# One weight chunk of projections moved between the heads of a sparse attention, linear attention moved one chunk earlier

## The chip, the cores and the metric

The kernel runs on one core of one Trainium2 chip. The core has five engines that run side by side and meet only at semaphores: TensorE (PE, with its weight loads listed as PEld), VectorE (DVE), ScalarE (ACT), GpSimd (POOL) and SyncE (SP), which issues most of the DMAs. The metric is the device time of one launch in microseconds (us); of several launches the median counts. Lower is better.

## The reference, cut to what matters

256 tokens of width 1024 pass through two blocks. Each block is a token mixer with a residual, and a mixture of 32 experts with a residual. Only the mixer of the first block is touched here:

```
hn = rms_norm(x, g_mix)
proj = hn @ w_in            # qa ka va ra alr | qb kb vb | qi ki wi | gate_a gate_b (1024 columns each)
ya = gla_mixer(qa, ka, va, ra, alr, ...) @ w_br_gla      # linear attention, 4 heads, 4 chunks of 64 tokens
yb = dsa_mixer(norm(qb), norm(kb), vb, qi, ki, wi, rel_bias) @ w_br_att   # sparse attention, 8 heads
mixed = sigmoid(gate_a) * ya + sigmoid(gate_b) * yb
x = x + mixed @ w_out
x = x + hier_moe(rms_norm(x, g_ffn), ...)
```

The linear attention has a state per chunk of tokens: the keys are decayed, k_dec^T v is formed for each chunk (the updates), the states are a running sum of the updates with a decay, and the outputs are q times the states, normed per head and multiplied by silu(ra). The sparse attention adds a bias by relative position and a mask of the 64 best keys to the scores, and takes a softmax over them.

## The kernel before, in words

Everything is float32. Each engine has its own program, written out by hand, and waits for named semaphores; there is no scheduler. Weights stream through a ring of six slots of 2 MB (`ring`), loaded by SP in one fixed order (`load`, issued at line 399); a load waits until the slot's last reader has passed (`s_used`). PE releases a slot with the first matmul that follows the last reader (`read[0]` in `mm`), so a slot comes free only when that next matmul has run. Three later loads go into the arena instead of the ring, and stand in the same SP order: w_gate of the second group of four experts waits for `s_gtp`, w_up of it for `s_on`, w_down of it for `s_mix`.

The projections of the first block come in chunks of 512 columns (numbers CH_QB to CH_GATE + 3). A gate chunk (`gate_chunk`) is 32 matmuls of 128x128 weights by 256 tokens; the profile lists each float32 matmul as two records, so 64. Its result fills two banks of PSUM (0 and 1, or 2 and 3), and ACT writes the sigmoid of it to `gate_a` or `gate_b` (line 851). The order on PE (lines 1882 to 1948) is:

- the chunk RA, gate chunk 0 (CH_GATE), the updates of the linear attention (waits for `s_kdec`), gate chunk 1, the outputs of the linear attention (waits for `s_st`, the states), gate chunk 2, the transposes of the normed outputs (waits for `s_gn`), gate chunk 3, the head transposes of the sparse attention's q and k, a wait for their copies (`s_hT_a`, `s_hT_d`) and for the last sigmoid, and the sparse attention.

The sparse attention is a loop over 16 (tile, head) pairs on PE, DVE and ACT. In step i PE makes the scores of pair i, transposes the probabilities of pair i - 2, runs what `beside_sparse(i)` puts there, and multiplies the probabilities of pair i - 3 by v. The piece beside is the product of the linear attention with w_br_gla (`gla_branch`): 24 of its 32 matmuls lie in the 16 steps, so one and two in turn, and 8 behind the loop. They write banks 6 and 7 or 3 and 4 by `beside_buf`; DVE multiplies each pair of results by `gate_a` (`mix_gla`, line 1309), two of the four inside the loop (behind its steps 7 and 12).

ACT's order is written out as well. After the silu of RA (line 841) ACT waits for `s_rel_dram`, which comes when a DMA that ACT issued at line 834 has landed: it writes a row of bias values, held in 8 partitions of SBUF, 128 times over to a scratch tensor in DRAM (2 MB). ACT then issues the two DMAs that read the bias back in its skewed form (line 846, `s_bias`), and takes the square root for the head norm (`root(ROOTS["dsa"])`, line 662). Only then come the sigmoids of the gate chunks.

DVE's order around this: the selection of the keys (`select(1)`), the decayed keys (line 1280, `s_kdec`), the norm of q and k of the sparse attention (`group_norm("dsa")`, lines 989, 990, 939, then 942 to 945 and 993 behind ACT's root), the states of the linear attention (lines 1289 and 1292, `s_st`), the norm of the linear attention's outputs (`group_norm("gla")`, the same lines, then 1302, `s_gn`), the copy of kT (line 1305), the loop of the sparse attention. POOL adds the masks to the bias when both bias DMAs have landed (line 609).

Behind the first mixer stand the out-product, router and experts of block one (lines 1175, 1181, 784 belong to them), then block two. Its experts have 6 MB of weights each.

Of the kernel before, what the change touches and what calls it, by code (L numbers as in the profile page):

```python
# [27 lines left out]
ACT = mybir.ActivationFunctionType  # L28
AX = mybir.AxisListType

P = 128
T, D = 256, 1024
TT = T // P
KD = D // P
# [81 lines left out]
def program(nc, a, out):  # L116

    with ExitStack() as ctx:
# [3 lines left out]
        def sem(name):  # L122
            return ctx.enter_context(nc.semaphore(name))
# [92 lines left out]
        def bank(b, n=512, o=0):  # L216
            return ps[:, b * 512 + o:b * 512 + o + n]
# [74 lines left out]
        s_otp = sem("out_transposed")  # L292
        s_oT = sem("out_T")
        s_br = sem("branch_product")
        s_mix = sem("branch_mixed")
# [61 lines left out]
        def slot3(s, k, n):  # L357
            return place(s)[:, 0:k * n].rearrange("p (k n) -> p k n", k=k)
# [158 lines left out]
        def tiles4(b0, n=4):  # L517

            return ps[:, b0 * 512:b0 * 512 + n * T].rearrange("p (m t) -> p m t", t=T)
# [9 lines left out]
        def beside_buf(i):  # L529

            return (6, 3)[i % 2]

# [124 lines left out]
        def _(act):  # L657
# [189 lines left out]
            root(ROOTS["dsa"])  # L847
            for n in range(4):
                gate = (gate_a, gate_b)[n // 2][:, 4 * (n % 2):4 * (n % 2) + 4, :]
                act.wait_ge(s_proj, CH_GATE + n + 1)  # L850
                act.activation(gate, tiles4(2 * ((CH_GATE + n) % 2)), ACT.Sigmoid).then_inc(s_pev_a, 1)
                if n == 1:
                    act.wait_ge(s_go, 1)
                    for i in range(2):
                        act.activation(og.rearrange("p t (n i e) -> p t n i e", n=2, i=2)[:, :, :, i],
                                       bank(6 + i).rearrange("p (t n e) -> p t n e", t=TT, n=2),
                                       ACT.Copy).then_inc(s_gog, 1)
                    root(ROOTS["gla"])
                if n == 2:
                    act.wait_ge(s_gtp, 1)  # L860
                    act.activation(gla_T, tiles4(4), ACT.Copy, scale=gcol[:, R_GLA:R_GLA + 1]).then_inc(s_gT, 1)
# [4 lines left out]
            act.wait_ge(s_otp, 1)  # L866
            act.activation(att_T, tiles4(4), ACT.Copy).then_inc(s_oT, 1)  # L867
            norm(1, R_FFN)
            act.wait_ge(s_rexp_in, 1)
# [52 lines left out]
        def _(dve):  # L922
            done = [0]

            def step(ins):

                done[0] += 1
                ins.then_inc(s_dve, 1)
                dve.wait_ge(s_dve, done[0])
# [377 lines left out]
            def mix_gla(n):  # L1307
                dve.wait_ge(s_br, n + 1)
                dve.tensor_tensor(mixT[:, 2 * n:2 * n + 2, :], tiles4(beside_buf(n), 2),
                                  gate_a[:, 2 * n:2 * n + 2, :], ALU.mult).then_inc(s_mix, 1)  # L1310

            def beside_sparse(i):
                if i in (7, 12):
                    mix_gla((7, 12).index(i))

# [3 lines left out]
            for n in range(4):  # L1319
                dve.wait_ge(s_br, 4 + n + 1)  # L1320
                gb = gate_b[:, 2 * n:2 * n + 2, :]
                step(dve.tensor_tensor(gb, tiles4(n, 2), gb, ALU.mult))
                dve.wait_ge(s_mix, n + 1)
                dve.tensor_tensor(mixT[:, 2 * n:2 * n + 2, :], mixT[:, 2 * n:2 * n + 2, :], gb,
                                  ALU.add).then_inc(s_mix, 1)
# [91 lines left out]
        def _(pe):  # L1417
# [477 lines left out]

            gate_chunk(CH_GATE)

            pe.wait_ge(s_kdec, 1)
# [9 lines left out]
            ins.then_inc(s_u, 1)  # L1908
            gate_chunk(CH_GATE + 1)
            pe.wait_ge(s_st, 1)  # L1910
# [6 lines left out]
            ins.then_inc(s_go, 1)  # L1917
            gate_chunk(CH_GATE + 2)
            pe.wait_ge(s_gn, 1)
            transposes(4, lambda m, tt: og[:, tt, m * P:(m + 1) * P], 4, s_gtp, 4)  # L1920
            gate_chunk(CH_GATE + 3)
            pe.wait_ge(s_hn, 1)
            pe.wait_ge(s_gT, 1)
            pe.wait_ge(s_gog, 2)
            head_transposes(q_tm, k_tm)
            pe.wait_ge(s_hT_a, 1)
            pe.wait_ge(s_hT_d, 1)
            pe.wait_ge(s_pev_a, CH_GATE + 4)
            w_bg = slot3(CH_BG, 4, D)

            def gla_branch(m, k):

                n = m // 2
                if m % 2 == 0 and k == 0 and n >= 2:
                    pe.wait_ge(s_mix, n - 1)
                ins = mm(bank(beside_buf(n), T, (m % 2) * T), w_bg[:, k, m * P:(m + 1) * P], gla_T[:, k, :], k == 0,
                         k == 3)
                if m % 2 == 1 and k == 3:
                    ins.then_inc(s_br, 1)

            def beside_sparse(i):

                if i < 16:
                    for t in range(i * 24 // 16, (i + 1) * 24 // 16):
                        gla_branch(t // 4, t % 4)

            arrived(CH_BG, 0)
            sparse_attention(beside_sparse)
            for m in (6, 7):
                for k in range(4):  # L1950
                    gla_branch(m, k)
            read[0] += 1
            pe.wait_ge(s_on, 2)
# [111 lines left out]
```

## Time and profile before

| | us |
|---|---|
| median of 3 runs | 1020.8 |
| lowest and highest run | 1019.43, 1023.84 |
| the profiled execution, its own time | 1014.91 |
| its span, first to last instruction | 1013.1 |
| PE busy in the span | 831.0 (82%) |
| DVE, ACT, POOL busy | 208.4, 172.4, 56.7 |
| mean granted clock of TensorE | 0.935 |

Times in the views are counted from the start of the span. "Busy" is time in instructions. A row of a timeline is a run of like instructions of one engine: start, length, engine, line, operation, written tile <- read tiles, shapes, count, and in brackets how long the engine sat idle before it and what ended that. A row of the stretches (A:B) gives for each engine its busy time and count, then the clock granted to TensorE as a share of full speed, the share of the DMA engines that was busy, and GB/s. SPq and ACTq are the issuing of DMAs on these engines' queues.

### The profile page before, as it was taken

What the parts mean: (1) busy time and instruction counts of PE and PEld (TensorE: products, weight loads), DVE (VectorE), ACT (ScalarE), POOL (GpSimd) and SP (SyncE); (2) the same over time, 40 slices, a digit from 0 to 9 for tenths busy, and PEclk for the clock granted to TensorE, in tenths of its full rate; (3) what the DMA queues carried; (4) which work ended last, traced back from release to release, by engine and by line L of the source; (5) the groups of instructions that cost most, each with busy time, mean ns of one, the idle gap of its engine ahead of it and who ended that gap; (6) DMA issues with size and microseconds to landing.
All of it is one profiled execution on the core that took longest, in us unless ns stands there. A gap on an engine that the chain in (4) does not pass through costs nothing.

```text
span 1013.1 us, 18784 instructions
## 1 busy us (share of the span) xinstructions
PE 831.0 (82%) x8295; PEld 536.5 (53%) x8295; DVE 208.4 (21%) x545; ACT 172.4 (17%) x386; POOL 56.7 (6%) x60
## 2 busy tenths in 40 slices
PE   5999999999989998999999896856657565675755
PEld 4546488776576665444665754452525334253541
DVE  2023515122332222044444210100001010010100
ACT  2012112330411114011653110001001000000100
POOL 8000003000002000043000000000000000000000
PEclk9999999999999999999999899888978798897978
DMA  9944675526276999444264899999999999999995
GB/s 268 368 167 150 109 234 184 217 91 241 89 289 262 407 408 388 175 167 166 83 234 161 320 426 413 426 423 421 428 411 429 418 427 421 419 427 412 433 415 205
DMA packets 67184, 307.30 MB, mean 303 GB/s; under 512 B 4528, under 2 KB 7688, under 8 KB 58952
## 3 DMA queue, kind: packets, MB, share of 16 engines
q1 hardware_dynamic: 62544, 301.85, 75.2%
q10 hardware_dynamic: 3256, 3.67, 2.2%
q0 software_dynamic: 1344, 1.20, 0.5%
q8 instruction: 30, 0.49, 0.2%
q14 instruction: 10, 0.08, 0.0%
HBM read 303.56 MB, written 3.15 MB: 303 GB/s over the span
## 4 chain that ended last, share of the span: by engine, by line
PE 59%; DMA 32%; SPq 3%; DVE 2%; ACT 2%; issue 1%; DVEq 0%; ACTq 0%
PE ps L1422 56%; DMA ring<-in_w_down 14%; DMA ring<-in_w_up 10%; DMA ring<-in_w_gate 7%; SPq L399 3%; PE ps L1448 1%; DMA xx<-in_x 1%; PE ps L1582 0%; PE ps L1545 0%; PE ps L1470 0%; DVE arena L1181 0%; ACT arena L784 0%; DVE xx L1209 0%; DVE xs L950 0%; ACT arena L720 0%
## 5 line engine op out<-in xcount | busy, mean ns | idle before, releaser
L1422 PE MATMUL ps<-ring,arena 128*32 128x128 f32 (+2 forms) x5520 | 290.5, 353 | 145.7 <-DMA ring<-in_w_down 61.4
L1422 PEld LDWEIGHTS ps<-ring,arena 128*32 128x32 f32 (+1 forms) x5520 | 179.7, 123 | 249.0 <-issue 91.2
L1422 PE MATMUL ps<-ring,xx 128*128 128x512 f32 (+2 forms) x416 | 167.0, 560 | 0.0
L1422 PE MATMUL ps<-arena 128*32 128x128 f32 (+10 forms) x752 | 117.2, 358 | 5.4 <-ACT arena L791 1.7
L1422 PEld LDWEIGHTS ps<-ring,xx 128*128 128x128 f32 x416 | 77.0, 193 | 84.3 <-issue 83.3
L1422 PEld LDWEIGHTS ps<-arena 128*128 128x128 f32 (+4 forms) x752 | 64.7, 154 | 39.1 <-issue 32.5
L1422 PE MATMUL ps<-xx,ring 128*128 128x256 f32 (+2 forms) x400 | 78.2, 382 | 0.0
L1422 PEld LDWEIGHTS ps<-xx,ring 128*128 128x128 f32 (+2 forms) x400 | 64.7, 175 | 12.9 <-issue 1.6
L1175 DVE TENSOR_TENSOR arena<-arena,ps 128x128 f32<-128x128 f32 x40 | 11.5, 288 | 282.5 <-ACT arena L771 282.5
L1422 PE MATMUL ps<-arena,xs 128*128 128x128 f32 x512 | 64.7, 287 | 1.9 <-DVE arena L1081 1.9
L1422 PEld LDWEIGHTS ps<-arena,xs 128*128 128x128 f32 x512 | 61.6, 201 | 6.7 <-issue 4.2
L771 ACT ACTIVATE arena<-ps 128x128 f32<-128x128 f32 x40 | 11.1, 278 | 306.8 <-PE ps L1422 306.8
L1193 DVE COPY arena<-ps 128x512 f32<-128x512 f32 x16 | 11.1, 692 | 171.8 <-PE ps L1422 171.8
L791 ACT ACTIVATE arena<-ps 128x512 f32<-128x512 f32 x16 | 9.6, 597 | 159.2 <-PE ps L1422 159.2
L1422 PE MATMUL ps<-arena,ring 128*128 128x256 f32 x128 | 30.9, 382 | 1.2 <-ACT arena L867 1.2
L1181 DVE TENSOR_TENSOR arena<-ps,gcol 128x512 f32<-128x512 f32 x32 | 22.1, 692 | 37.6 <-PE ps L1422 37.6
L1422 PE MATMUL ps<-ring,xs 128*128 128x512 f32 x64 | 27.8, 592 | 0.0
L1422 PEld LDWEIGHTS ps<-arena,ring 128*128 128x128 f32 x128 | 23.3, 194 | 4.0 <-issue 1.4
L1422 PEld LDWEIGHTS ps<-ring,xs 128*128 128x128 f32 x64 | 12.1, 190 | 14.4 <-issue 14.3
L1702 PE MATMUL ps<-const,arena 128*128 128x128 f32 x40 | 13.7, 343 | 4.4 <-DVE arena L1175 4.0
L1448 PE MATMUL ps<-const,xs 128*128 128x128 f32 x32 | 5.6, 346 | 12.4 <-DVE xs L950 12.4
L609 POOL TENSOR_TENSOR arena<-arena 128x1024 f32<-128x1024 f32 (+1 forms) x2 | 7.8, 3918 | 136.2 <-DMA arena<-bias_scratch 136.2
(246 smaller groups left out, 514.8 us busy)
## 6 DMA issues: line engine op xcount, KB each, us to landing
ring<-in_w_gate SPq DMA_DIRECT2D x38, 2048.0 KB, 22.8
ring<-in_w_up SPq DMA_DIRECT2D x38, 2048.0 KB, 23.1
ring<-in_w_down SPq DMA_DIRECT2D x37, 2048.0 KB, 24.2
ring<-in_w_in SPq DMA_DIRECT2D x16, 2048.0 KB, 18.5
ring<-in_w_out SPq DMA_DIRECT2D x4, 2048.0 KB, 7.9
arena<-in_w_gate SPq DMA_DIRECT2D x2, 2048.0 KB, 10.3
arena<-in_w_up SPq DMA_DIRECT2D x2, 2048.0 KB, 9.1
arena<-in_w_down SPq DMA_DIRECT2D x2, 2048.0 KB, 7.8
```

The lines of the kernel that those rows point to most:

```text
L399: sp.dma_start(dst, src).then_inc(s_extra[s] if s < 0 else s_slot[s % RING], 16)
L609: pool.tensor_tensor(bm[tt], bm[tt], pick_mask[:, tt:tt + 1, 0:nk].broadcast_to([P, AH, nk]), ALU.add).then_inc(s_bm, 1)
L771: act.activation(silu_g[:, j % 2], bank(6, P), ACT.Silu).then_inc(s_silu[b], 1)
L791: act.activation(y_sb[:, 0:512], bank(4), ACT.Copy).then_inc(s_ysb_a[b], 1)
L1175: dve.tensor_tensor(hid_tm[:, j % 2], silu_g[:, j % 2], bank(7, P), ALU.mult).then_inc(s_h[b], 1)
L1181: dve.tensor_tensor(xg[:, 4 * half:4 * half + 4, :], bank(6 + half).rearrange("p (k s) -> p k s", k=4), gains, ALU.mult).then_inc(s_xg[b], 1)
L1193: dve.tensor_copy(y_sb[:, 512:1024], bank(5)).then_inc(s_ysb_d[b], 1)
L1422: ins = pe.matmul(dst, w, x, start=start, stop=stop, skip_group_check=True)
L1448: ins = pe.transpose(bank(b0 + m // 2, P, (m % 2) * T + tt * P), src(m, tt), ident)
L1702: pe.transpose(bank(4, P, j * P), hid_tm[:, j % 2], ident).then_inc(s_ht[b], 1)
```

## The change

The last gate chunk (gate chunk 3) leaves its place ahead of the head transposes. 8 of its 32 matmuls run behind the head transposes, ahead of the wait for the copies of q and k; the other 24 run in steps 0 to 7 of the sparse attention, three in each. The 24 matmuls of the linear attention's product that were spread over the 16 steps are now in steps 8 to 15, three in each. The gate's results are written to bank 3 and bank 6, copied raw to `gate_b` by DVE behind its steps 4 and 9, and turned into a sigmoid by ACT in place, after the transposed attention output. The two multiplications by gate_a in the loop move to DVE's steps 12 and 15. The updates of the linear attention run ahead of gate chunk 0 instead of behind it, its outputs ahead of gate chunk 1, its transposes ahead of gate chunk 2. On ACT the copies of the linear attention's outputs stand behind the sigmoid of gate chunk 0, and that of the transposed ones behind gate chunk 1. SP's program is not touched.

```diff
@@ buffers of the pieces beside the heads
-            return (6, 3)[i % 2]
+            return (3, 6)[i % 2]
@@ ACT
-            for n in range(4):
+            for n in range(3):
                 gate = (gate_a, gate_b)[n // 2][:, 4 * (n % 2):4 * (n % 2) + 4, :]
                 act.wait_ge(s_proj, CH_GATE + n + 1)
                 act.activation(gate, tiles4(2 * ((CH_GATE + n) % 2)), ACT.Sigmoid).then_inc(s_pev_a, 1)
-                if n == 1:
+                if n == 0:
                     act.wait_ge(s_go, 1)
...
                     root(ROOTS["gla"])
-                if n == 2:
+                if n == 1:
                     act.wait_ge(s_gtp, 1)
                     act.activation(gla_T, tiles4(4), ACT.Copy, scale=gcol[:, R_GLA:R_GLA + 1]).then_inc(s_gT, 1)
...
             act.activation(att_T, tiles4(4), ACT.Copy).then_inc(s_oT, 1)
+            act.wait_ge(s_gcp, 2)
+            act.activation(gate_b[:, 4:8, :], gate_b[:, 4:8, :], ACT.Sigmoid).then_inc(s_pev_a, 1)
@@ DVE
+            def copy_gate(half):
+                if half == 0:
+                    dve.wait_ge(s_gate, 1)
+                else:
+                    dve.wait_ge(s_proj, CH_GATE + 4)
+                dve.tensor_copy(gate_b[:, 4 + 2 * half:6 + 2 * half, :],
+                                tiles4(beside_buf(half), 2)).then_inc(s_gcp, 1)
+
             def beside_sparse(i):
-                if i in (7, 12):
-                    mix_gla((7, 12).index(i))
+                if i in (4, 9):
+                    copy_gate((4, 9).index(i))
+                if i in (12, 15):
+                    mix_gla((12, 15).index(i))
...
                 dve.wait_ge(s_br, 4 + n + 1)
                 gb = gate_b[:, 2 * n:2 * n + 2, :]
+                if n == 2:
+                    dve.wait_ge(s_pev_a, CH_GATE + 4)
@@ PE
-            gate_chunk(CH_GATE)
-
             pe.wait_ge(s_kdec, 1)
...
             ins.then_inc(s_u, 1)
-            gate_chunk(CH_GATE + 1)
+            gate_chunk(CH_GATE)
             pe.wait_ge(s_st, 1)
...
             ins.then_inc(s_go, 1)
-            gate_chunk(CH_GATE + 2)
+            gate_chunk(CH_GATE + 1)
             pe.wait_ge(s_gn, 1)
             transposes(4, lambda m, tt: og[:, tt, m * P:(m + 1) * P], 4, s_gtp, 4)
-            gate_chunk(CH_GATE + 3)
+            gate_chunk(CH_GATE + 2)
...
             head_transposes(q_tm, k_tm)
-            pe.wait_ge(s_hT_a, 1)
-            pe.wait_ge(s_hT_d, 1)
-            pe.wait_ge(s_pev_a, CH_GATE + 4)
+            arrived(CH_GATE + 3, 0)
+            w_gate3 = slot3(CH_GATE + 3, KD, 512)
             w_bg = slot3(CH_BG, 4, D)
 
+            def last_gate(t):
+
+                m, k = t // KD, t % KD
+                ins = mm(bank(beside_buf(m // 2), T, (m % 2) * T), w_gate3[:, k, m * P:(m + 1) * P], xnT[:, k, :], k == 0,
+                         k == KD - 1)
+                if (m, k) == (1, KD - 1):
+                    ins.then_inc(s_gate, 1)
+                if (m, k) == (3, KD - 1):
+                    ins.then_inc(s_proj, 1)
+
             def gla_branch(m, k):
 
                 n = m // 2
-                if m % 2 == 0 and k == 0 and n >= 2:
-                    pe.wait_ge(s_mix, n - 1)
+                if m % 2 == 0 and k == 0:
+                    if n < 2:
+                        pe.wait_ge(s_gcp, n + 1)
+                    else:
+                        pe.wait_ge(s_mix, n - 1)
...
             def beside_sparse(i):
 
                 if i < 16:
-                    for t in range(i * 24 // 16, (i + 1) * 24 // 16):
-                        gla_branch(t // 4, t % 4)
-
+                    for t in range(3 * i, 3 * i + 3):
+                        if t < 24:
+                            last_gate(8 + t)
+                        else:
+                            gla_branch((t - 24) // 4, (t - 24) % 4)
+
+            pe.wait_ge(s_pev_a, CH_GATE + 3)
+            for t in range(8):
+                last_gate(t)
+            pe.wait_ge(s_hT_a, 1)
+            pe.wait_ge(s_hT_d, 1)
             arrived(CH_BG, 0)
             sparse_attention(beside_sparse)
...
-            read[0] += 1
+            read[0] += 2
```

## Rows read from the trace of the kernel before

**Rows 1.** Page: the chain that ended last, by engine; then a piece of it.

```profile
PE 59%; DMA 32%; SPq 3%; DVE 2%; ACT 2%; issue 1%; DVEq 0%; ACTq 0%
...
189.97 1.15 issue
```

**Rows 2.** Timeline of PE from RA's end to the first head.

```profile
129.02 13.98 PE L1422 MATMUL ps<-xx,ring 128*128 128x256 f32 x64
142.93 1.15 PE L1422 MATMUL ps<-arena 64*64 64x128 f32 x32
...
158.02 1.16 PE L1422 MATMUL ps<-arena 64*64 64x128 f32 x32
...
187.71 1.91 PE L1448 MATMUL ps<-const,arena 128*128 128x128 f32 x16
191.12 0.46 PE L1422 MATMUL ps<-arena 64*128 64x128 f32 x2 [1.50 <-issue]
```

**Rows 3.** Timeline of DVE: head norm behind the root, states, norm of the linear outputs.

```profile
148.76 0.35 DVE L942 RECIPROCAL stat<-stat 128x32 f32<-128x32 f32 x1 [21.98 <-ACT stat L662]
...
152.49 2.26 DVE L1292 SCALAR_TENSOR_TENSOR arena<-arena,stat,ps 128x128 f32<-128x128 f32 x6
160.34 2.53 DVE L989 TENSOR_TENSOR xs<-arena 128x1024 f32<-128x1024 f32 x1 [5.59 <-ACT arena L855]
...
164.17 3.13 DVE L939 TENSOR_SCALAR stat<-stat 128x32 f32<-128x32 f32 x1
167.59 0.35 DVE L942 RECIPROCAL stat<-stat 128x32 f32<-128x32 f32 x1 [0.30 <-ACT stat L662]
...
169.91 1.23 DVE L1302 TENSOR_TENSOR arena<-arena 128x1024 f32<-128x1024 f32 x1
```

**Rows 4.** Timeline of ACT and its queue: the bias DMAs, the load ahead of the root.

```profile
146.17 1.01 ACTq L846 DMA_DIRECT2D arena<-bias_scratch  x2
147.21 1.28 ACT L662 ACT_TABLE_LOAD   x1 [16.96 <-issue]
```

**Rows 5.** Stretch with the bias write alone in flight; columns as in rows 7.

```profile
104.00:108.00 4.00, 4.00 (x10) 1.71 (x9) 0.00 (x0) 0.00 (x0) 0.00 (x0) 1.00 0.46 49
```

**Rows 6.** Timeline of PE in the loop: the transposes that begin steps 10, 11, 12.

```profile
210.27 0.44 PE L1545 MATMUL ps<-const,arena 128*128 128x128 f32 x2
...
212.09 0.44 PE L1545 MATMUL ps<-const,arena 128*128 128x128 f32 x2
...
214.34 0.44 PE L1545 MATMUL ps<-const,arena 128*128 128x128 f32 x2
```

**Rows 7.** The loop: us, then PE, PEld, DVE, ACT, POOL busy, clock, DMA share, GB/s.

```profile
191.10:219.70 28.60, 28.58 (x153) 21.91 (x153) 8.01 (x36) 12.60 (x49) 0.00 (x0) 1.00 0.32 131
```

**Rows 8.** Timeline of PE: the same work after a pause, and without one.

```profile
12.40 3.65 PE L1448 MATMUL ps<-const,xs 128*128 128x128 f32 x16 [12.40 <-DVE xs L950]
...
16.70 1.27 PE L1422 MATMUL ps<-xx,ring 128*128 128x256 f32 x3
...
279.67 5.47 PE L1422 MATMUL ps<-arena,xs 128*128 128x128 f32 x32 [0.96 <-DVE arena L1081]
...
293.25 3.84 PE L1422 MATMUL ps<-arena,xs 128*128 128x128 f32 x32
```

**Rows 9.** A stretch behind that pause; columns as in rows 7.

```profile
282.00:283.00 1.00, 1.00 (x7) 1.00 (x7) 0.38 (x3) 0.00 (x0) 0.00 (x0) 0.50 1.01 406
```

**Rows 10.** Timeline of POOL: the masks added to the bias.

```profile
159.45 7.81 POOL L609 TENSOR_TENSOR arena<-arena 128x1024 f32<-128x1024 f32 x2 [136.22 <-DMA arena<-bias_scratch]
```

**Rows 11.** Timeline of SP's queue, and PE's first use of expert weights.

```profile
188.02 0.37 SPq L399 DMA_DIRECT2D ring<-in_w_up  x1
...
285.91 3.70 PE L1422 MATMUL ps<-ring,arena 128*32 128x128 f32 x128 [0.56 <-DVE arena L1181]
```

**Rows 12.** Waits: engine, line, what it waited for, us in total, times, longest.

```profile
ACT arena L735 <- DVE xx L1331: 27.2, 1, 27.2
```

**Rows 13.** The chain in order of time, late in the run: start, us, what.

```profile
628.69 24.09 DMA ring<-in_w_up
```

More of the change, by code:

```diff
@@ L293, in program @@
         s_oT = sem("out_T")
+        s_gate = sem("first_half_of_last_gate")
+        s_gcp = sem("last_gate_copied")
         s_br = sem("branch_product")
```

## The prediction

> **What bounds the kernel now.** I read the chain that ended last first. PE holds 59% of it and DMA 32%, all others little [rows 1]. The DMA part lies in the second block's experts, where pieces like one of 24.09 us stand in the chain [rows 13]; ahead of them PE's own work is the chain. Those late loads start when PE frees their slots, so a time that PE loses or wins in the first mixer, at 129 to 230 us, should reach the end whole. Next I read PE's timeline of the part that is reordered. From 129.02 PE runs without a gap through the gate chunks and the two small products of the linear attention at 142.93 and 158.02; the one idle time is 1.50 us ahead of the first head at 191.12 [rows 2]. It is a piece of the chain: 1.15 us of it has no work behind it at all [rows 1]. Then the loop: 28.58 of 28.60 us of PE busy [rows 7]. So there is nearly nothing to fill on PE, and the question is what the new order makes PE wait for. That needs the timelines of DVE and ACT. DVE sits idle for 21.98 us, up to 148.76, waiting for ACT's square root, and makes the states of the linear attention only behind that, up to 152.49 + 2.26 = 154.75 [rows 3]. ACT in turn is idle for 16.96 us ahead of the load for that root, and leaves when it can issue the bias reads at 146.17 [rows 4], which is when the bias write has landed. Before, PE asks for the states at 158.02, 3.2 us after they are there: the late root costs nothing.
>
> **The updates, ahead of gate chunk 0.** They need the decayed keys; DVE had been idle since 126.8 when the root came [rows 3], so these were done before RA ended at 129.02. The updates keep their 1.15 us and do not wait. Nothing won, nothing lost.
>
> **The outputs, one chunk sooner.** PE will be ready for them at 129.02 + 1.15 + 13.91 (gate chunk 0, from 129.02 to 142.93 in rows 2) = 144.1. The states come at 154.75, plus 0.1 for the semaphore. Nothing in the change moves the write of the bias, ACT's order ahead of the root, or DVE's order. PE stands still for **10.8 us**. Queued behind this wait is everything: gate chunk 1 and 2, the transposes, the heads. DVE and ACT have nothing to do either in that time that they had not before. The write runs at 49 GB/s with 0.46 of the engines even when it is alone [rows 5], so it does not profit from an emptier queue; the one load that is now later, the first of w_out (its slot is freed by the first output matmul), overlapped it for the last 3 us only. I bound that gain by 0.4 us and take none.
>
> **The clock.** The pause is longer than any that I find inside this mixer. What pauses do: behind an idle time of 0.96 us ahead of 279.67 [rows 8], and others just before it, the granted clock was 0.50, the 1.2 GHz level [rows 9], and 32 records took 5.47 us against 3.84 for the same work later [rows 8], so 1.63 us were lost. After 12.40 us of idle at the start, 16 transposes took 3.65 us [rows 8] against 1.91 [rows 2], and matmuls still took 1.27 us for 3 at 16.70 where 64 take 13.98; full speed came at about 17.1. That is 1.74 for the transposes and some 0.65 for three matmuls: 2.4. The new pause is nearest to this one, so I take **2.4 us**, with 1.6 as the lower bound and twice 2.4 as the upper. The Trainium skill, in TensorE: Matmul & The Clock Gate, section Part 1: The HAM clock gate, has the half clock as the default state that activity lifts, which speaks against any change that makes a pause; the trace agrees, and the page's way of costing it, half of the slow time, gives the same order.
>
> **The norm of the linear outputs.** PE finishes gate chunk 1 at 154.85 + 1.16 + 13.98 + 2.4 = 172.4 and then waits for it. ACT copies the outputs from about 156.1 on (158.4 with the slow clock), and DVE starts at about 158.5 instead of 160.34. From DVE's start to its end it took 10.8 us [rows 3]; two pieces of it, 2.53 us for the multiplication and 3.13 us for an operation on 32 values, were long because POOL was adding the masks just then, from 159.45 for 7.81 us [rows 10]. With one load less ahead of them the bias reads land earlier, between 155 and 159.5. If POOL starts just ahead of DVE the whole 7.81 us fall on it: 158.3 + 7.8 + 1.2 + 1.2 + 0.5 + 3.55 (from the reciprocal at 167.59 to the end at 171.14) = 172.6. So this wait is 0 to 0.2 us, **0** in the sum; if the clock did not fall it would be up to 2.6 instead of the 2.4 of the clock, not on top of it. The Trainium skill, in SBUF — State Buffer, section SBUF: two separate sides, says that DVE and POOL take their shared port as a lock for a whole instruction; the two long DVE pieces agree, each ending as a POOL addition ends. By that rule the bound just given is the worst, and the sum stays as it is.
>
> **The last gate chunk.** PE does the same 32 matmuls elsewhere. Removed from its place: 13.8 us. 8 of them behind the head transposes cost 8 x 0.437 = 3.5 us (13.98 for 64 records, 32 matmuls, [rows 2]) and cover the 1.50 us idle time: kT's copy, which PE waited for, is then done. Gain **1.5 us**. The other 24 in the loop: a step with one matmul beside takes 212.09 - 210.27 = 1.82 us, one with two 214.34 - 212.09 = 2.25 [rows 6], so one more costs 0.43, its full price; nothing in a step hides it. 24 x 0.43 = 10.3, and 3.5 + 10.3 = 13.8: a move at no gain. The lower bound of what the loop hides is 0.02 us [rows 7].
>
> **What goes with it.** DVE gets two copies of some 0.7 us in the loop and is busy for 8.01 of 28.60 us there [rows 7]; PE waits for the first from step 8 on, DVE makes it in step 4; the second is made in step 9 for step 10 or 11. Behind each copy on DVE stand the next logits, due two steps later. Cost 0; without this cover, 1.4. ACT's one sigmoid and its table load, some 2.3 us (1.28 for a load in rows 4), lie ahead of ACT's next norm, for which it waited 27.2 us [rows 12], and DVE needs the result only for its third product, behind half of the attention's branch. Cost 0. SP: the slot of the last gate chunk comes free only behind the loop, so the load of w_up that went out at 188.02, and behind it in SP's order the second w_gate, go out at about 234. The experts use them from 285.91 on [rows 11], then 12 us later; 8 MB are queued there, some 20 us at the 406 GB/s of rows 9. Cost 0; 40 us of cover.
>
> **Sum.** + 10.8 + 2.4 - 1.5 = **+11.7 us**. The profiled execution, 1014.9, would become 1026.6. It lies 5.9 us below the median of the runs, 1020.8, with the same program; I add the difference to the median: **1032.5 us**, 1.1% slower.
>
> **Rivals.**
> 1. The clock stays low for longer, since the output products are small: twice the price, +14.1, 1034.9. For it: no row shows a restart on small products. Against it: each slow stretch that I read ended by itself under 5 us of work.
> 2. The loop hides the 24 matmuls (waits between engines take in the time): + 11.7 - 10.3 = +1.4, 1022.2, no change. It decides if a step with three matmuls beside takes less than 2.25 + 0.43. Against it: rows 6 and 7.
> 3. The other side: the states are there in time. If the bias write landed 10.8 us sooner than here, near 135, PE would never wait; left is the gain at the heads, -1.5, 1019.3, not slower. It is a single place, ACT's wait at line 842; each us by which the write is early takes one from the pause. For it: one execution is a thin base. Against it: the rate of 49 GB/s looks fixed, and it began before anything that the change touches.
> 4. Both, 2 and 3: -11.8, 1009.0, faster.
> 5. The change doesn't do what it says: the chunk's matmuls would have to stand elsewhere on PE, which its program excludes; no chance of its own.
>
> **How the numbers follow.** Forecast 0.78, rival 1 0.09, rival 2 0.06, rival 3 0.05, rival 4 0.02. A measurement of this kernel can tell about 0.5%, 5.1 us, from no change. Slower by more: forecast and rival 1, 0.87. Within it: rivals 2 and 3, 0.11. Faster by more: 0.02. The range has to hold 8 in 10: the forecast with its bounds (stall 10.4 to 10.8, clock 1.6 to 2.4) is +10.5 to +11.9, rival 1 reaches +14.1, and the medians of runs that spread over 4.4 us add about 3 on each side. 1027 to 1038.
>
> **What would show it.** Right: PE idle for 10 to 11 us ahead of the output products, ended by DVE's line of the states; the clock at 0.50 behind it; no idle time ahead of the first head; the loop at 28.6 + 10.3 = 38.9 us; DVE still idle for 22 us up to about 148.8. Wrong: PE's outputs starting before 150, or a loop of under 36 us, or the part from RA's end to the loop's end less than 9 us longer than its 90.6 us. If that part is 11 us longer but the end is not, the step that failed is that PE's delay reaches the end whole.

## The result and the profile after

| | before | after |
|---|---|---|
| median of 16 runs each, us | 1020.33 (1014.85 to 1023.84) | 1027.32 (1025.11 to 1029.73) |
| ratio, 95% interval | | 1.0076 [1.0059, 1.0092] |
| profiled execution, us | 1014.9 | 1029.73 |
| its span, us, and mean granted clock | 1013.1 | 1027.9, 0.928 |
| RA's end to the start of the attention's branch, us | 96.2 | 109.4 |

The kernel is slower, by 7.0 us at the median (the interval is 6.0 to 9.4 us) where 11.7 were forecast; the time lies 0.3 us above the low end of the range. Lines of the new kernel are numbered higher: the matmul helper is L1438 (L1422), the states L1296 (L1292), the root L664 (L662). In the kernels of the experiments they stand some 4 to 8 lines further down: the matmul helper is L1446 in the variants of the changed kernel and L1430 in those of the kernel before, the states are L1304 and L1300.

The page of the changed kernel, its span and its chain by engine:

```profile
span 1027.9 us, 18788 instructions
...
PE 53%; DMA 38%; DVE 2%; SPq 2%; ACT 2%; issue 1%; ACTq 0%; DVEq 0%
```

PE held 59% of the chain before and DMA 32% [rows 1]. The bias write has entered the chain, and PE follows behind it. The chain of the changed kernel in order of time, two of its links:

```profile
99.92 48.51 DMA bias_scratch<-arena
...
157.10 17.84 PE ps L1438 x96
```

The timeline of PE in the changed kernel, RA's end to the first steps behind the heads (start, us, instructions, idle time before and what ended it):

```profile
130.00 1.15 PE L1438 MATMUL ps<-arena 64*64 64x128 f32 x32
131.09 14.08 PE L1438 MATMUL ps<-xx,ring 128*128 128x256 f32 x64
157.10 2.04 PE L1438 MATMUL ps<-arena 64*64 64x128 f32 x32 [11.93 <-DVE arena L1296]
159.07 15.88 PE L1438 MATMUL ps<-xx,ring 128*128 128x256 f32 x64
174.78 1.04 PE L1464 MATMUL ps<-const,arena 128*128 128x128 f32 x8
...
191.22 3.62 PE L1438 MATMUL ps<-xx,ring 128*128 128x256 f32 x16
194.76 0.49 PE L1438 MATMUL ps<-arena 64*128 64x128 f32 x2
```

Read it against rows 2. The updates stand right behind RA, as forecast, and do not wait; behind gate chunk 0 PE is idle for 11.93 us, ended by DVE's line of the states. The output products take 2.04 us instead of 1.16, the next chunk 15.88 instead of 13.98. The transposes of the linear outputs at 174.78 don't wait. The eight matmuls of the last chunk stand at 191.22 and the first head follows with no idle time. The clock and the traffic behind the pause, then the loop, as rows 7 give them (us; PE, PEld, DVE, ACT, POOL; clock; DMA share; GB/s):

```profile
160.00:161.00 1.00, 1.00 (x4) 0.74 (x3) 0.70 (x1) 0.98 (x2) 1.00 (x1) 0.50 0.97 358
161.00:163.00 2.00, 2.00 (x7) 1.61 (x6) 2.00 (x1) 0.57 (x1) 2.00 (x1) 0.56 1.05 410
163.00:170.00 7.00, 7.00 (x34) 6.17 (x33) 6.00 (x9) 1.51 (x2) 0.14 (x1) 1.00 0.30 110
194.80:233.70 38.90, 38.90 (x201) 30.96 (x201) 9.21 (x38) 12.43 (x48) 0.00 (x0) 1.00 0.06 22
```

The granted clock is at 0.50, the 1.2 GHz level, until about 162.8 (worked out from the 0.56 of 161 to 163), and full from then on. The loop holds 38.90 us of PE without a gap.

What DVE and ACT did meanwhile (timelines of the changed kernel):

```profile
151.05 0.35 DVE L946 RECIPROCAL stat<-stat 128x32 f32<-128x32 f32 x1 [23.38 <-ACT stat L664]
...
154.78 2.27 DVE L1296 SCALAR_TENSOR_TENSOR arena<-arena,stat,ps 128x128 f32<-128x128 f32 x6
160.30 3.92 DVE L993 TENSOR_TENSOR xs<-arena 128x1024 f32<-128x1024 f32 x1 [3.26 <-ACT arena L857]
...
168.31 1.23 DVE L1306 TENSOR_TENSOR arena<-arena 128x1024 f32<-128x1024 f32 x1
```

```profile
148.45 1.02 ACTq L848 DMA_DIRECT2D arena<-bias_scratch  x2
149.50 1.28 ACT L664 ACT_TABLE_LOAD   x1 [18.36 <-issue]
```

This is rows 3 and 4 again. The states end at 157.05, 2.3 us later than before, because the write landed 2.3 us later: it was issued 0.6 us later and took 48.51 us, against 46.9 (99.28 to 146.17) before. All of the 13.2 us that the part from RA's end to the branch is longer is now named: 11.93 of pause, 0.88 + 1.80 of low clock (against 1.16 and the 14.08 that the chunk ahead of the pause took), less 1.5 at the heads, is 13.1. The delay reaches the end: the span is 14.8 us longer.

### The profile page after: what moved, and what is told of

It is laid out like the page before. It is cut to its first block, busy times and chain, and to the rows that moved or that the text cites. A ratio compares the mean times of both kernels' runs of the same rounds, so it can differ in the third digit from the quotient of the medians.

```text
span 1027.9 us, 18788 instructions
## 1 busy us (share of the span) xinstructions
PE 836.2 (81%) x8295; PEld 541.2 (53%) x8295; DVE 208.0 (20%) x547; ACT 173.6 (17%) x387; POOL 55.7 (5%) x60
## 4 chain that ended last, share of the span: by engine, by line
PE 53%; DMA 38%; DVE 2%; SPq 2%; ACT 2%; issue 1%; ACTq 0%; DVEq 0%
PE ps L1438 50%; DMA ring<-in_w_up 14%; DMA ring<-in_w_down 14%; DMA bias_scratch<-arena 5%; DMA ring<-in_w_gate 5%; SPq L401 2%; PE ps L1464 1%; DMA xx<-in_x 1%; PE ps L1598 0%; PE ps L1561 0%; PE ps L1486 0%; ACT arena L786 0%; DVE xx L1213 0%; DVE xs L954 0%; ACT arena L722 0%
## 5 line engine op out<-in xcount | busy, mean ns | idle before, releaser
L1438 PE MATMUL ps<-ring,arena 128*32 128x128 f32 (+2 forms) x5520 | 288.1, 351 | 143.1 <-DMA ring<-in_w_down 60.2
L1438 PEld LDWEIGHTS ps<-ring,arena 128*32 128x32 f32 (+1 forms) x5520 | 178.9, 122 | 244.8 <-issue 92.3
L1438 PE MATMUL ps<-ring,xx 128*128 128x512 f32 (+2 forms) x416 | 170.9, 570 | 0.0
L1438 PE MATMUL ps<-arena 128*32 128x128 f32 (+10 forms) x752 | 118.5, 374 | 17.9 <-DVE arena L1296 11.9
L1438 PEld LDWEIGHTS ps<-ring,xx 128*128 128x128 f32 x416 | 78.8, 198 | 86.2 <-issue 85.3
L1438 PEld LDWEIGHTS ps<-arena 128*128 128x128 f32 (+4 forms) x752 | 66.4, 162 | 51.5 <-issue 32.7
L1438 PE MATMUL ps<-xx,ring 128*128 128x256 f32 (+2 forms) x400 | 80.7, 386 | 0.0
L1438 PEld LDWEIGHTS ps<-xx,ring 128*128 128x128 f32 (+2 forms) x400 | 65.1, 178 | 12.7 <-issue 1.3
L1438 PE MATMUL ps<-arena,xs 128*128 128x128 f32 x512 | 64.4, 286 | 1.8 <-DVE arena L1085 1.8
L1438 PEld LDWEIGHTS ps<-arena,xs 128*128 128x128 f32 x512 | 61.3, 200 | 5.8 <-issue 3.4
L1438 PE MATMUL ps<-arena,ring 128*128 128x256 f32 x128 | 29.4, 380 | 1.2 <-ACT arena L869 1.2
L1438 PE MATMUL ps<-ring,xs 128*128 128x512 f32 x64 | 27.8, 592 | 0.0
L1438 PEld LDWEIGHTS ps<-arena,ring 128*128 128x128 f32 x128 | 23.7, 191 | 4.2 <-issue 1.4
L1438 PEld LDWEIGHTS ps<-ring,xs 128*128 128x128 f32 x64 | 12.1, 190 | 14.4 <-issue 14.3
```

Source lines behind the costliest of these rows:

```text
L1438: ins = pe.matmul(dst, w, x, start=start, stop=stop, skip_group_check=True)
```

## The experiments

Two theories stood against each other. **R** (late root): ACT waits for the bias write ahead of a square root that has nothing to do with it, so the states come at a fixed time, and PE, now earlier, waits. Its rival puts the loss in the placement: outputs between the chunks, the slow clock itself, or the loop. A second pair was about size: **C**, that the kernel before pays for its 1.50 us pause ahead of the heads [rows 2] with more than its length, in granted clock, against the plain sum. All experiments hold each engine's count of expert rounds, which is read from memory, at 1 or more, by one register operation per engine. The kernel before and the changed one with that alone show what it costs. The cuts of the edits below leave it out; they are against the changed kernel, or against the kernel before where the heading names it.

**The kernel before, again.** Expected:

> The kernel before, with one register operation per engine more: the count of rounds that is read from memory is held at 1 or above (all kernels of these experiments have it). Expected by every theory: ratio 1.000 within 0.3%, PE idle 1.5 us ahead of the first head and 0 ahead of the output products. It is also a second look at the kernel before: its profiled execution was at 1015 while its median is at 1020. If the bias write lands later in the slower executions (theory L), the states come up to 3 us later there with no pause on PE; if it is the late weight stream that varies (theory W), everything up to the end of the sparse loop agrees with the first profile within 1 us and the difference lies behind 600 us.

Measured: 1020.17 us (1014.63 to 1023.67), ratio 1.0001 [0.9976, 1.0026]. The register operation costs nothing that shows. The profiled execution took 1023.57 us with a span of 1021.7, 8.6 us above that of the other. The difference is mostly clock. Nearly the same work of the second block, in both (a stretch of the kernel before, then of the kernel before again):

```profile
496.10:506.10 10.00, 10.00 (x73) 7.62 (x71) 5.39 (x30) 7.85 (x32) 0.00 (x0) 1.00 0.02 5
```

```profile
498.50:508.50 10.00, 10.00 (x47) 8.26 (x46) 3.11 (x21) 4.77 (x23) 0.00 (x0) 0.55 0.19 79
```

PE is busy in all of both, but does 47 instructions in place of 73. By the timelines of PE the same instructions stand 0.8 us later in the second execution at RA's end, 2.4 us behind the first block's attention, 4.1 near 480, 8.7 at 509, and the spans differ by 8.6. The steps lie where the clock is at 0.50 in the second execution alone: 3.4 us behind 193, 3.4 us near 406, and some 10 us from 497 to 507, which cost 1.6, 1.7 and 4.6 us. So such a stretch costs about half its length. The first of them lies just behind the short pause (timeline of PE, then a stretch, kernel before again):

```profile
191.89 0.46 PE L1430 MATMUL ps<-arena 64*128 64x128 f32 x2 [1.50 <-issue]
```

```profile
194.00:195.00 1.00, 1.00 (x4) 0.53 (x2) 0.00 (x0) 0.25 (x2) 0.00 (x0) 0.50 1.00 406
```

So the kernel before is a mixture: of 96 executions of it, 35 lie under 1017 us and 58 at 1019 or above. The profiled execution that the prediction was made against belongs to the first group, the median to the second. Neither theory of the expectation explains it: the bias reads went out 1.25 us later (147.42 against 146.17), with no pause ahead of the output products, and the difference lies ahead of 600 us.

**The changed kernel, again** (one execution). Expected:

> The changed kernel, a second profile. Theory R (the late root on ScalarE, behind the bias write, makes the states late): a pause of 10.5 to 12.5 us ahead of the output products, the clock at 0.50 behind it, the part from RA's end to the loop's end 102 to 104 us. The rival (the pause of the first profile was a chance of one execution): a pause under 8 us.

Measured: 1024.98 us, span 1023.2. In the timeline of PE the pause is 10.35 us, just under the 10.5 expected at least, and the slow clock behind it costs 1.4 us:

```profile
154.70 2.04 PE L1446 MATMUL ps<-arena 64*64 64x128 f32 x32 [10.35 <-DVE arena L1304]
156.67 14.63 PE L1446 MATMUL ps<-xx,ring 128*128 128x256 f32 x64
```

The bias reads went out at 146.06 here, and the outputs start 8.64 us behind that; in the first execution it was 148.45 and 8.65. So the pause ends with the landing of the write, some 8.65 us behind it.

**Root first.** The direct test of R: the same work, the root ahead of the wait for the write.

```diff
             act.activation(ra, ..., ACT.Silu).then_inc(s_pev_a, 1)
+            root(ROOTS["dsa"])
             act.wait_ge(s_rel_dram, 16)
...
-            root(ROOTS["dsa"])
             for n in range(3):
```

> The changed kernel with ScalarE's square root for the head norm put ahead of its wait for the bias write instead of behind it. Theory R: the states are ready near 139, no pause ahead of the output products, the clock stays at 1.00, so 10.8 to 11.9 us of pause and 2.4 to 2.7 us of slow clock go; a new wait for the norm of the linear outputs of 0 to 5 us can take their place, because VectorE's norm then meets GpSimd's masks. From RA's end to the loop's end 89 to 94 us; 9 to 14 us faster than the changed kernel, ratio to before 0.998 to 1.003. The rival (VectorE's own work or the updates make the states late, not the root): the pause keeps 8 us or more and the ratio stays at 1.0076.

Measured: **1013.65 us** (1009.39 to 1021.09), ratio to before 0.9943 [0.9917, 0.9970]; 13.7 us below the changed kernel, and faster than both kernels. The gain on the changed kernel is as expected; the ratio lies below the 0.998 to 1.003 that was. The timelines of PE and of DVE:

```profile
130.19 14.08 PE L1446 MATMUL ps<-xx,ring 128*128 128x256 f32 x64
144.20 1.15 PE L1446 MATMUL ps<-arena 64*64 64x128 f32 x32
145.28 14.08 PE L1446 MATMUL ps<-xx,ring 128*128 128x256 f32 x64
```

```profile
131.81 0.35 DVE L952 RECIPROCAL stat<-stat 128x32 f32<-128x32 f32 x1 [5.04 <-ACT stat L668]
...
135.53 2.27 DVE L1304 SCALAR_TENSOR_TENSOR arena<-arena,stat,ps 128x128 f32<-128x128 f32 x6
```

The states end at 137.8, PE asks at 144.2, the pause is gone, and with it the slow products. RA's end to the branch is 94.7 us: 96.2 less the 1.5 of the heads. By that plain sum the median would be 1.5 us under the kernel before; it is 6.6 under it.

**The early root in the kernel before.** If the root were worth something by itself, it would show here.

```diff
+            root(ROOTS["dsa"])
             act.wait_ge(s_rel_dram, 16)
...
-            root(ROOTS["dsa"])
             for n in range(4):
```

> The kernel before with ScalarE's root ahead of its wait for the bias write, the fourth corner of the square of both orders on both engines. Theory R: the states are ready 12 to 14 us earlier, near 146 behind the updates of 143, but PE asks for them at 158 as before, so nothing moves on PE: from RA's end to the attention's branch 96.2 to 98 us, ratio 0.998 to 1.002. The rival (the early root by itself is what made the mended kernel faster than before): ratio 0.996 or less.

Measured: 1020.52 us (1014.68 to 1031.03), ratio 1.0000 [0.9973, 1.0027]. Timelines of DVE and of PE:

```profile
145.22 2.26 DVE L1300 SCALAR_TENSOR_TENSOR arena<-arena,stat,ps 128x128 f32<-128x128 f32 x6
```

```profile
158.65 1.15 PE L1430 MATMUL ps<-arena 64*64 64x128 f32 x32
...
191.75 0.46 PE L1430 MATMUL ps<-arena 64*128 64x128 f32 x2 [1.50 <-issue]
```

The states end at 147.5, some 7 us sooner than in rows 3 (they now wait for the updates), but PE asks at 158.65 as before; the 1.50 us pause stayed. RA's end to the branch took 99.4 us, 3.1 more than in rows 2, because the clock is at 0.50 from about 193 to 199, behind that pause. With the three kernels above this closes a square: the early root is worth 0 within 2.8 us in the old order and 13.7 us in the new one. R is shown.

**The gate chunk moved, the linear attention where it was.** The half of the change that fills the pause at the heads, without the half that makes the new one.

```diff
-                if n == 0:
+                if n == 1:
                     act.wait_ge(s_go, 1)
...
-                if n == 1:
+                if n == 2:
                     act.wait_ge(s_gtp, 1)
...
+            gate_chunk(CH_GATE)
             pe.wait_ge(s_kdec, 1)
...
-            gate_chunk(CH_GATE)
+            gate_chunk(CH_GATE + 1)
             pe.wait_ge(s_st, 1)
...
-            gate_chunk(CH_GATE + 1)
+            gate_chunk(CH_GATE + 2)
             pe.wait_ge(s_gn, 1)
             transposes(...)
-            gate_chunk(CH_GATE + 2)
             pe.wait_ge(s_hn, 1)
```

> One part of the change alone: the last gate chunk between the heads, its sigmoid behind them, but the updates, outputs and transposes of the linear attention behind gate chunks 0, 1 and 2 as before. Theory R: PE asks for the states at 158 as before, no pause there, no slow clock; 1.5 us won ahead of the first head, 1 to 1.5 us lost where the head transposes now follow directly on the linear attention's and wait for their copy. Ratio 0.998 to 1.002, loop 38.9 us, RA's end to the loop's end 89.5 to 91 us. The rival (three matmuls beside each head are what costs): this kernel is as slow as the changed one, 1.006 or more.

Measured: 1015.14 us (1011.96 to 1016.71), ratio 0.9952 [0.9928, 0.9976], below the 0.998 to 1.002 expected. The rival fell: the three matmuls beside each head fill the loop as in the changed kernel, and the kernel is not slow. RA's end to the branch took 96.2 us, no less than before: it wins the 1.50 us at the heads and pays for a new short wait a little earlier, behind the transposes of the linear outputs (timeline of PE):

```profile
159.01 1.15 PE L1446 MATMUL ps<-arena 64*64 64x128 f32 x32
...
174.01 1.04 PE L1472 MATMUL ps<-const,arena 128*128 128x128 f32 x8
...
176.34 1.94 PE L1472 MATMUL ps<-const,arena 128*128 128x128 f32 x16 [1.29 <-issue]
```

Yet the median fell by 5.1 us, and none of 11 executions reached 1019. In this kernel a pause of nearly the same length, followed by other work, does not bring the upper group. The plain sum has no room for that.

**The pause filled with spare work.** This parts the pause from its clock. PE gets 24 matmuls whose result nobody reads.

```diff
             gate_chunk(CH_GATE)
+            for k in range(24):
+                mm(bank(6, T), xnT[:, k % KD, 0:P], xnT[:, k % KD, :], True, True)
             pe.wait_ge(s_st, 1)
```

> The changed kernel with 24 spare matmuls of 128x128 by 256 (10.5 us, results unused) between gate chunk 0 and the wait for the states. The pause is full of work now, but the states come no earlier. Theory K (of the changed kernel's loss, 1.4 to 2.7 us are the half clock behind the pause): the outputs take 1.16 us instead of 2.04, gate chunk 1 takes 14.0 instead of 14.6 to 15.9, from RA's end to the attention's branch 104.5 to 106 us instead of 106.5 and 109.4, ratio to before 1.004 to 1.006. The rival (the slow stretch comes from something other than the pause): both stay as slow as in the changed kernel, and the ratio stays at 1.0076 or above.

Measured: 1024.48 us (1021.35 to 1028.98), ratio 1.0061 [1.0036, 1.0085], 2.8 us below the changed kernel (1.8 if each is taken against the kernel before as measured beside it, 1019.28 and 1020.33). Timeline of PE:

```profile
145.79 10.52 PE L1446 MATMUL ps<-xx 128*128 128x256 f32 x48
156.24 1.15 PE L1446 MATMUL ps<-arena 64*64 64x128 f32 x32
157.32 14.08 PE L1446 MATMUL ps<-xx,ring 128*128 128x256 f32 x64
```

The spare work stands in place of the idle time, so all that can be saved is the clock: the outputs take 1.15 us in place of 2.04, the chunk 14.08 in place of 15.88 or 14.63. RA's end to the branch is 105.1 us, and 96.2 + 10.5 - 1.5 is 105.2. In this execution the states were ready at 154.6, some 1.6 us before the spare work ended, so the pause would have been 8.8 us and the filling gave part of the clock's gain away.

This trace holds something else that bears on C. Near 510 the clock is at 0.50 for about 10 us, at the same work as in the kernel before again, though PE has no idle time ahead of the outputs or of the heads here (a stretch of it):

```profile
510.00:511.00 1.00, 1.00 (x6) 0.97 (x5) 0.00 (x0) 0.42 (x3) 0.00 (x0) 0.50 0.00 0
```

It is the longest execution of this kernel, 4.5 us above its median. The long stretch near 500 does not need idle time of PE ahead of the heads.

**The short pause of the kernel before, filled**, measured twice. The test of C:

```diff
             head_transposes(q_tm, k_tm)
+            for k in range(4):
+                mm(bank(2, T), xnT[:, k, 0:P], xnT[:, k, :], True, True)
             pe.wait_ge(s_hT_a, 1)
```

> The kernel before with 4 spare matmuls (1.75 us, results unused) in its one pause, the 1.50 us ahead of the first head. In the second profile of the kernel before the clock fell to 0.50 at 193.7 just behind this pause and the loop took 1.6 us more; in the first it did not. Theory C (the median of before holds such a slow stretch, and the two kernels that lose the pause win it back on top of their 1.5 us): the loop never slows, ratio 0.997 to 0.999. The rival (the pause is harmless and the wins of 5 us have their source behind the mixer): ratio 1.000 to 1.001.

> The kernel before with its short pause filled, measured once more since its interval reached 1.0001. Theory C: ratio 0.996 to 0.999, no or nearly no executions above 1019 where about two in three of the kernel before are. The rival: ratio 0.999 to 1.001 with the same share of slow executions as before.

Measured: 1015.54 us, ratio 0.9977 [0.9952, 1.0001], and 1015.87 us, ratio 0.9975 [0.9952, 0.9999]. The timeline of PE and the stretch behind it, in the first of them:

```profile
190.09 1.89 PE L1430 MATMUL ps<-xx 128*128 128x256 f32 x8
191.91 0.48 PE L1430 MATMUL ps<-arena 64*128 64x128 f32 x2
```

```profile
194.00:195.00 1.00, 1.00 (x6) 0.55 (x5) 0.05 (x1) 0.31 (x2) 0.00 (x0) 1.00 1.01 410
```

The spare work takes 1.89 us where the idle time took 1.50, so by the plain sum this kernel is 0.4 us slower. It is 3.6 to 3.7 us faster at the median and 2.3 to 2.4 at the mean, and of its 24 executions none reached 1019, where 58 of 96 of the kernel before did. The intervals end at 1.0001 and 0.9999; the missing upper group is the stronger evidence. But the filled kernel is not the lower group alone: 6 of its 24 executions lie at 1017.5 to 1018.3, where the kernel before has 1 of 96. In the two executions that were profiled the clock is full where it was 0.50 above, in the attention and around 500 us. They are two of the 24, and the mean granted clock of all 24 is 0.930, while in the 80 executions of the kernel before whose clock is on record it is 0.934 under 1017 us and 0.927 at 1019 or above. That the filling takes time off is shown; that it does so through the stretches near 500 is not.

**The short pause put back**, in the changed kernel and in the one with the root first: the two waits of the first head stand again ahead of the eight matmuls.

```diff
-            for t in range(8):
-                last_gate(t)
             pe.wait_ge(s_hT_a, 1)
             pe.wait_ge(s_hT_d, 1)
+            for t in range(8):
+                last_gate(t)
```

> The changed kernel with the wait for the copies of q and k back ahead of the 8 matmuls of the last gate chunk, so that the pause of 1.5 us ahead of the heads is there again; the long pause ahead of the outputs stays. Theory C (that short pause costs more than its length in most executions, through the clock here and later in the run; this is why the changed kernel lost 7 us and not the 11.7 of the forecast): median 3 to 5 us above the changed kernel's 1027.3, ratio 1.010 to 1.013. The rival (the short pause costs its 1.5 us, and the difference to the forecast lies elsewhere): 1028 to 1029, ratio 1.009.

> The same for the changed kernel with the early root, which has no pause in the mixer at all (median 1013.7, ratio 0.9943). Theory C: the short pause takes back most of its 5.8 us, median 1017 to 1020, ratio 0.998 to 1.001, with executions above 1019. The rival: 1.5 us more, median 1015, ratio 0.996.

Measured: 1029.6 us (1028.44 to 1037.15) in six runs, ratio 1.0136 [1.0088, 1.0184]; and 1014.54 us (1012.77 to 1017.57), ratio 0.9965 [0.9940, 0.9989]. Timeline of PE, root first with the pause:

```profile
175.10 3.69 PE L1446 MATMUL ps<-xx,ring 128*128 128x256 f32 x16 [1.54 <-DVE arena L1317]
```

The pause is back at 1.54 us, and with the root first it costs 0.9 us, or 1.6 with each taken against the kernel before as measured beside it; C had it bring several. C as it was stated, that any such pause ahead of the heads brings the upper group, fell. In both kernels the eight matmuls, products of 256 columns, follow the pause; in the kernel before it is the first head's small products (64 rows, 128 columns). The changed kernel with the pause is slower by 2.3 us (3.1 in the same way), but on six runs, two of which lie at 1036 and above; its interval holds both what C and what the rival expected, and I read nothing from its size. The kernel that would tell, the pause directly ahead of the first head in the new order, was not tried.

## Why the prediction was right in sign and too high in size

- **The late root decides: right.** It named DVE's states behind ACT's root behind the bias write, and a pause of 10.8 us. Three executions show 11.93, 10.35 and, with the short pause put back, 8.84 us (timeline below). The chunk between took 14.08 us and the outputs began 8.65 us behind the bias reads in all three; what moves is the landing of the write, 146.06 or 148.45, and RA's end, 129.3 to 130.8. So the stated bounds, 10.4 to 10.8, held in none of the three.

```profile
154.71 2.04 PE L1446 MATMUL ps<-arena 64*64 64x128 f32 x32 [8.84 <-DVE arena L1304]
156.68 16.10 PE L1446 MATMUL ps<-xx,ring 128*128 128x256 f32 x64
```

- **Clock behind the pause, 2.4 us: right in kind and size, not in its bounds.** 2.7 and 1.4 in the two executions of the changed kernel, 2.9 behind the 8.84 us above, where 1.6 to 2.4 were the bounds; between the medians 1.8 to 2.8 when the pause was filled. The price does not go with the length of the pause. Rival 1, 4.8, did not occur. One of the rows that it was priced from, the start of the kernel [rows 8], has long durations only: the stretches of that time list the clock at 1.00. The Trainium skill, in TensorE: Matmul & The Clock Gate, section Part 1: The HAM clock gate, has activity lift the half clock; the spare matmuls, whose results nobody reads, agree: 1.15 us for the outputs behind them, 2.04 behind idle time.
- **Norm of the linear outputs, 0: right.** It ended at 169.5, PE asked at 174.8. The collision with POOL stayed inside its bound. Timeline of POOL in the changed kernel:

```profile
156.34 6.80 POOL L611 TENSOR_TENSOR arena<-arena 128x1024 f32<-128x1024 f32 x2 [133.13 <-DMA arena<-bias_scratch]
```

  DVE's multiplication began inside it, at 160.30, and ended at 164.22, 1.08 us behind it, 3.92 us long; with the root first, where DVE was done before POOL began, the same one took 1.23. The prediction has both long DVE pieces of the kernel before end as an addition ends. Only the second did; the multiplication ended at 162.87, 1.07 us behind the end of the first addition (159.45, 2.35 us long), so it seems to have begun to run there. The Trainium skill, in SBUF — State Buffer, section SBUF: two separate sides, has the port as a lock for a whole instruction, and this agrees.
- **The loop hides nothing: right.** Three matmuls beside a step give steps of 2.69 us where the forecast was 2.25 + 0.43, and 38.90 us where 38.9 were forecast. Rivals 2 and 4 fell with this. Timeline of PE, the transposes of three steps, to be held against rows 6:

```profile
224.40 0.44 PE L1561 MATMUL ps<-const,arena 128*128 128x128 f32 x2
...
227.09 0.44 PE L1561 MATMUL ps<-const,arena 128*128 128x128 f32 x2
...
229.77 0.44 PE L1561 MATMUL ps<-const,arena 128*128 128x128 f32 x2
```

- **Late weights, the copies, the sigmoid, 0: right.** Timeline of SP's queue and of PE at the first expert:

```profile
237.52 0.37 SPq L401 DMA_DIRECT2D ring<-in_w_up  x1
```

```profile
300.96 3.70 PE L1438 MATMUL ps<-ring,arena 128*32 128x128 f32 x128 [0.56 <-DVE arena L1185]
```

  The load went out 49.5 us later than in rows 11 and PE came there 15.05 us later, and its wait is the same 0.56 us.
- **The delay reaches the end: right** in the pair of profiled executions, with 13.2 us at the branch, 15.05 at the first expert and 14.8 in the span.
- **The states in time (rival 3): did not occur by itself,** and root first is that case made on purpose. It was priced at -1.5 and gave -6.6 at the median.
- **The step that was off: "I add the difference to the median".** The sum was made against one execution of 1014.9 us and laid onto a median of 1020.8 as if both stood for the same program at the same clock. The sentence in the prediction even gives the 5.9 us between them, and asks nothing of it. Against the group of executions to which the profiled one belongs, near 1015, the changed kernel costs 12.3 us, and 11.7 were forecast; but that group is picked after the result, and set against all executions of the changed kernel. Against the median it costs 7.0. The mis-sized term is **"Gain 1.5 us"** at the heads: it is 1.5 by the timeline (94.7 against 96.2), and filling the same pause in the kernel before took off 3.7 us more with spare work that is 0.4 us longer than the idle time, so 4.1 beyond the plain sum. +10.8 + 2.4 - 1.5 - 4.1 is +7.6, with 7.0 measured. The 4.1 is carried over from another kernel: in the new order, with other work behind the pause, putting it back cost 0.9 to 1.6 us.
- **Luck in the time.** 1027.3 is inside the range by 0.3 us. The range reaches down to 1027 by the 3 us added for the spread of the medians; the bounds of the mechanism alone, +10.5 to +11.9 on 1020.8, do not hold it. The base was 0.5 us high as well, 1020.8 from 3 runs against 1020.33 from 16.

What stays open is how filling that pause takes 3.7 us off the median. That low-clock stretches make up the difference between two executions of one kernel is shown step by step. That with the pause ahead of that work more executions are long is shown by filling it: 58 of 96 reach 1019 us, against 0 of 24. That the pause causes the stretches near 500 us, 300 us later, is not shown: the changed kernel with its pause filled has the same stretch with no idle time ahead of the heads. Which property of the work behind the pause matters is not shown either, nor whether it is the idle time or the 0.4 us by which the heads start later that counts: no kernel with the pause merely lengthened was tried. Nor is it shown that the 24 executions without an upper group would stay so at other times.

## What to carry to other kernels

Before a consumer is moved earlier, find its producer's slack on every in-order engine, down to the wait that stands in front of an unrelated instruction: here a square root behind a DMA's semaphore was free for one order, cost 13.7 us in the next, and one moved line gave it back. Before a sum is laid onto a median, ask which of the executions the profiled one is; where it lies some tenths of a per cent off, take a second profile and compare the granted clock stretch by stretch before a cause is named. A short idle time of PE can be worth more than its length, as one did here, so where spare work costs as much as the wait it fills, it is worth a try.

## What the runs showed of the hardware

- The granted clock of one program differs from execution to execution with PE busy throughout: 1.00 and 0.55 over 10 us of nearly the same work in the second block. In the one pair compared, three such stretches cost 1.6, 1.7 and 4.6 of the 8.6 us between the spans. The times of the kernel before fall into groups near 1015, 1020 and 1023.7 us.
- 1.89 us of spare matmuls in place of 1.50 us of idle time took 3.7 and 3.6 us off the median. I had not expected spare work to pay at that size.
- Behind idle times of PE of 8.84, 10.35 and 11.93 us the half clock cost 2.9, 1.4 and 2.7 us.
- The bias write took 48.5 and 46.8 us in two executions of the changed kernel, and its landing moved by 2.4 us (148.45 and 146.06, by the reads that wait for it); whatever waits for it inherits that.
